# Two transformer blocks in one kernel: unit-matrix products without a use are left out

## The chip, the cores and the metric

One core of a Trainium2 chip. The metric is the device time of one execution in microseconds. Before the change three runs took 3058.13, 3059.27 and 3061.95 us; their median is 3059.27.

## What is computed

Two blocks of two layers each work on one sequence of 512 tokens with 1024 channels, all in float32. The first block's layer is

```
h = rmsnorm(x);  proj = h @ w_in
y_a = gated_delta_branch(...)     # 8 heads, chunks of 64, both directions
y_b = diff_attention_branch(...)  # 8 heads, softmax minus lambda * softmax
x = x + (sigmoid(gate_a) * (y_a @ w_pa) + sigmoid(gate_b) * (y_b @ w_pb)) @ w_out
```

and after its two layers comes a final RMS norm. The second block's layer is

```
z = rms(x) @ w_in
y = concat(windowed attention (8 heads), forgetting attention (4), mLSTM (4))
x = x + y @ w_out
x = x + square(relu(rms(x) @ w_ff1)) @ w_ff2
```

The products that the change leaves out are part of none of this.

## The kernel before

Everything is held transposed: channels on the 128 partitions, tokens along the free dimension. x is eight tiles of 128 x 512. Weights come through `Stream` (line 210): a chunk of 1 MB is loaded, ScalarE rounds it to float32r (the high part), VectorE subtracts to get the low part, and TensorE makes three products of 512 columns per tile: high times high, high times low, low times high (lines 319, 322 and 323, in `Stream.product`).

The program is a sequence of stages, each a Block of its own. At the end of a Block all engines meet, and none goes on before the last has come; this text calls it a border. The order is: start (line 572), then for each layer of the first block delta, merge, attention (`diff_phase`), merge, output; then the final norm; then for each layer of the second block attention (`attention2_phase`) and output with feed-forward (`out_ff_phase`). Some of the next stage's products are pulled ahead of the border, and weights of the next stage are loaded and split before it.

Within a stage TensorE's instructions run in the order in which they are written. Where a long stream of weight products can be cut into pieces, it is a generator, `fill`, and `some(fill, n)` puts n pieces of it between the products of a head, so that TensorE has work while the other engines do theirs. `first_chunk` (line 329) is the start of a stage: its step t takes tile t of the normed h as soon as VectorE has its low part (line 532), two output banks at a time, with a pair of gate products between.

The row sums of the RMS norm are products with a matrix of ones. In the start and in the final norm there are eight of 512 columns (line 431), each behind a square of ScalarE (line 427), with two buffers for the squares. In the output stages GpSimd adds the first squares up (line 465), and TensorE makes two products of 256 columns from the sum (line 470) and two from the last square (line 475); ScalarE then takes logarithm and exponential (lines 483 and 486).

`idle_products` (line 688) makes n products of the unit matrix with itself, 128 columns each, in float32, into a bank that the next real product overwrites or that is free at that point. Nobody reads them. They stand in TensorE's order without any wait of their own, at these places:

- start: 6 behind the row sums (line 605)
- final norm: 8 ahead of the sums and 5 behind them (lines 664 and 667)
- merge: 4 at the end (line 786), four times in the program
- output stage of the first block: 5 at the end (line 946), twice
- feed-forward, first layer of the second block only: 8 ahead of the sums for the next norm and 5 behind them (lines 1044 and 1047)
- delta: 6 (first layer) or 4 (second layer) at the beginning (line 1741), and 5 in the first head, ahead of the wait for the matrix that is to be transposed (line 1646)
- attention of the first block: 4 ahead of the last unit's wait for its weights (line 2273), where a unit is 128 queries of one head
- attention of the second block: 6 at the beginning and 4 at the end (lines 2876 and 2932)

That is 106 products in 21 places.

Of the kernel before, what the change touches and what calls it, by code (L numbers as in the profile page):

```python
# [14 lines left out]
P = 128  # L15
# [556 lines left out]
def start_phase(k, xT_in, positions, cc_in, cx_in, following, pairs, gate_weights):  # L572
# [4 lines left out]
    with ExitStack() as ctx:  # L577
        pos = k.sb(ctx, "pos", [P, SEQ], I32)
        ang = k.sb(ctx, "ang", [P, SEQ], F32)
        tmp = k.sb(ctx, "tmp", [P, 3, SEQ], F32)  # L580
        stats = RowStats(k, k.sb(ctx, "sq", [P, 2, SEQ], F32), 4)
        MAGIC = 1.5 * 2.0 ** 23
        C1 = 6.28125
        C2 = float(np.float32(2 * math.pi - C1))
        C3 = float(2 * math.pi - C1 - float(np.float32(2 * math.pi - C1)))
        with nc.Block() as block:
            @block.sync
            def _(sp):
                sp.dma_start(k.xT[:, :, :], xT_in).then_inc(loaded, 16)
                sp.dma_start(k.cc[:, :], cc_in).then_inc(loaded, 16)  # L590
                sp.dma_start(k.cx, cx_in).then_inc(loaded, 16)
                sp.dma_start(pos[:, :], positions.partition_broadcast(P)).then_inc(loaded, 16)
                gw.load(sp)
                following.prefetch(sp)
                for dst, src in pairs:
                    sp.dma_start(dst, src).then_inc(consts, 16)
                sp.wait_ge(loaded, 64)
                sp.wait_ge(consts, 16 * len(pairs))

            @block.tensor  # L600
            def _(pe):
                pe.wait_ge(loaded, 64)
                for t in range(KT):
                    stats.sum(pe, t)
                idle_products(k, pe, 0, 6)

            @block.vector
            def _(dve):
                chain = Chain(dve, stepd)
                dve.wait_ge(loaded, 64)  # L610
                chain(dve.tensor_copy(tmp[:, 0], pos[:, :]))
                chain(dve.tensor_scalar(ang[:, :], tmp[:, 0], k.cx[:, CX_INVF:CX_INVF + 1], None, ALU.mult))

                for w, shift in enumerate((0.0, math.pi / 2)):
                    chain(dve.tensor_scalar(tmp[:, 0], ang[:, :], 1.0 / (2 * math.pi), shift / (2 * math.pi), ALU.mult, ALU.add))
                    chain(dve.tensor_scalar(tmp[:, 1], tmp[:, 0], MAGIC, None, ALU.add))
                    chain(dve.tensor_scalar(tmp[:, 0], tmp[:, 1], MAGIC, None, ALU.subtract))
                    chain(dve.scalar_tensor_tensor(tmp[:, 1], tmp[:, 0], -C1, ang[:, :], ALU.mult, ALU.add))
                    chain(dve.scalar_tensor_tensor(tmp[:, 1], tmp[:, 0], -C2, tmp[:, 1], ALU.mult, ALU.add))
                    chain(dve.scalar_tensor_tensor(tmp[:, 1], tmp[:, 0], -C3, tmp[:, 1], ALU.mult, ALU.add))  # L620
                    dst = k.sin1 if w == 0 else k.cos1
                    chain(dve.tensor_scalar(tmp[:, 1], tmp[:, 1], shift, math.pi, ALU.add, ALU.min))
                    dve.tensor_scalar(dst[:, :], tmp[:, 1], -math.pi, None, ALU.max).then_inc(posf, 1)
                    dve.wait_ge(posf, w + 1)
                gw.low(dve)
                following.first_low(dve)

            @block.scalar
            def _(act):
                act.preload_act_table_set(LN_EXP)  # L630
                act.wait_ge(loaded, 64)
                for t in range(KT):
                    stats.square(act, t)
                gw.high(act)
                following.first_high(act)
                stats.finish(act)
# [4 lines left out]
def final_norm_phase(k, fn, gain, pairs, gate_weights):  # L641
# [5 lines left out]
    with ExitStack() as ctx:  # L647
        stats = RowStats(k, k.sb(ctx, "sq", [P, 2, SEQ], F32), 4)
        with nc.Block() as block:
# [11 lines left out]

            @block.tensor
            def _(pe):
                idle_products(k, pe, 0, 8)
                for t in range(KT):
                    stats.sum(pe, t)
                idle_products(k, pe, 0, 5)

            @block.scalar
            def _(act):  # L670
# [12 lines left out]
                gw.low(dve)  # L683
                dve.wait_ge(prod, KT)
    k.next_phase()


def idle_products(k, pe, bank, n):

    for _ in range(n):  # L690
        pe.matmul(k.bank[bank][:, 0:P], k.ident, k.ident, start=True, stop=True)


def gate_product(k, pe, w, width, bank, t):
# [48 lines left out]
def merge_phase(k, st, following, yS, macc, mS, begun, pairs=(), angles=()):  # L743
# [5 lines left out]
    with ExitStack() as ctx:  # L749
# [3 lines left out]
        with nc.Block() as block:  # L753
# [12 lines left out]
            @block.tensor  # L766
            def _(pe):
                pe.sem_inc(tile, 1)
                for c in range(2):
                    st.ready(pe, 0, c)  # L770
                    out = k.bank[2 + c if c else begun][:, :]
                    steps = tuple(range(KT)) if c else (KT - 1,)
                    whole(st.product(pe, out, c, 1, yS, frees=c == 1, steps=steps, begin=c == 1)).then_inc(tile, 2 - c)

                with pe.Fori(1, KT // 2) as i:
                    for c in range(2):
                        st.ready(pe, i, c)

                        pe.wait_ge(mul, nth(i, 2, c))
                        whole(st.product(pe, k.bank[c][:, :], c, 0, k.hT)).then_inc(tile, 1)  # L780
                        whole(st.product(pe, k.bank[2 + c][:, :], c, 1, yS)).then_inc(tile, 1)
                if mS is not None:

                    pe.wait_ge(mul, 2 + KT - 1)
                    drain(first_outputs(k, pe, following, OUT_BANKS_MERGE, mS, MERGE_FIRST, lambda t: pe.wait_ge(mul, 3 + t)))
                idle_products(k, pe, 7, 4)

            @block.scalar
            def _(act):
# [139 lines left out]
def out_phase(k, st, following, aS, sq, banks, left, pairs=(), gate_weights=None):  # L929

    out = OutStage(k, st, following, aS, sq, banks + banks, left, pairs, gate_weights)
    with k.nc.Block() as block:
# [9 lines left out]
        @block.tensor  # L942
        def _(pe):
            out.tensor(pe)
            out.sums(pe)
            idle_products(k, pe, 7, 5)

        @block.scalar
        def _(act):
# [20 lines left out]
def out_ff_phase(k, st_out, aS, sq, left, st, following, gain_of, gate_weights=None, pairs=(), result=None):  # L970
# [9 lines left out]
    with ExitStack() as ctx:  # L980
# [5 lines left out]
        with nc.Block() as block:  # L986
# [23 lines left out]
            def _(pe):  # L1010
# [10 lines left out]
                def second(i, c, last_panel):  # L1021
# [16 lines left out]
                    if last_panel and c == 3:  # L1038
# [2 lines left out]
                                step(kk, n)  # L1041
                        if stats:
                            pe.wait_ge(relu, 4 + 4 * NP)
                            idle_products(k, pe, 2, 8)
                            stats.gathered_sum(pe)
                            stats.last_sum(pe)
                            idle_products(k, pe, 2, 5)
                        return
                    for kk in range(4):
                        if c == 2:  # L1050
# [244 lines left out]
def delta_phase(k, st, following, l, pA, cg, tab, lam, yS, wsp, odd, few):  # L1295
# [23 lines left out]
    with ExitStack() as ctx:  # L1319
# [73 lines left out]
        with nc.Block() as block:  # L1393
# [139 lines left out]
            def _(pe):  # L1533
# [108 lines left out]
                def core(i, p, first=False, ahead=2):  # L1642
                    fill = stream(i, ahead)
                    some(fill, 3 if first else 1)
                    if first:
                        idle_products(k, pe, AB + 1, 5)
                    pe.wait_ge(nn_ready, i + 1)
                    for c in range(NS):
                        last = pe.transpose(B[AB][:, c * P:(c + 1) * P], Nn[:, c], k.ident)
# [88 lines left out]
                        turn_out(i, i, "out")  # L1738
                        drain(fill)

                idle_products(k, pe, YB + 1, 4 if l else 6)
                st.ready(pe, 0, 0)
                for last in first_chunk(st, pe, (B[0][:, :], B[1][:, :]), k.hT, norm.ready(pe), gates.product(pe)):
                    last.then_inc(tile, 1)
# [394 lines left out]
def diff_phase(k, st, following, lam, yS, odd):  # L2139
# [22 lines left out]
    with ExitStack() as ctx:  # L2162
# [10 lines left out]
        UNITS1 = HEADS * NTOK  # L2173
# [4 lines left out]
        with nc.Block() as block:  # L2178
# [39 lines left out]
            def _(pe):  # L2218
# [50 lines left out]
                def turn_weights(u):  # L2269
                    if u > 0:  # L2270
                        pe.wait_ge(at_ready, u)
                    if u == UNITS1 - 1:
                        idle_products(k, pe, TB, 4)
                    pe.wait_ge(a_ready, u + 1)
                    for c in range(NTOK):
                        last = pe.transpose(B[TB][:, c * P:(c + 1) * P], A[:, u % 2, c * P:(c + 1) * P], k.ident)
# [403 lines left out]
def attention2_phase(k, st, following, pB, cb, col, yS, wsp, bones, caus, few):  # L2680
# [38 lines left out]
    with ExitStack() as ctx:  # L2719
# [38 lines left out]
        with nc.Block() as block:  # L2758
# [41 lines left out]
            def _(pe):  # L2800
# [72 lines left out]
                                             vtm[:, m % 2, kb, 64 * h:64 * h + 64], start=(y == 0), stop=(y == len(ks) - 1))  # L2873
                    last.then_inc(pv_ready, 1)

                idle_products(k, pe, TB + 1, 6)
                st.ready(pe, 0, 0)
                for last in first_chunk(st, pe, (B[GB], B[GB + 1]), k.hT, norm_in.ready(pe), gates.product(pe)):
                    last.then_inc(g_ready, 1)
# [49 lines left out]
                values(UNITS - 1)  # L2929
                drain(fill)  # L2930
                turn_out(TILES - 1)
                idle_products(k, pe, TB, 4)

            @block.scalar
            def _(act):
# [491 lines left out]
```

## Time and profile before

| what | value |
|---|---|
| median of three runs | 3059.27 us |
| the profiled execution | 3057.0 us |
| its span, first to last instruction | 3055.1 us |
| mean granted clock of TensorE | 0.999 |
| TensorE matmul busy | 2959.6 us, 97% |
| VectorE busy | 1722.9 us, 56% |
| ScalarE busy | 1422.7 us, 47% |
| GpSimd busy | 414.2 us, 14% |
| start stage | 0 to 24.6 us |
| first block, two layers | to 1807 us |
| final norm | to 1819.7 us |
| second block, two layers | to the end |

Busy is the time in which at least one instruction of the engine runs; a matmul's end is modelled, so that a row of eight matmuls in a sequence seems to overlap with the next. The granted clock is that of TensorE's array as a share of 2.4 GHz: 1.00 is 2.4 GHz, 0.50 is 1.2 GHz. All times in the rows are microseconds from the first instruction.

### The profile page before, as it was taken

Reading aid. Unit: us, or ns where it says so; the run is one execution under the profiler, and the core shown is the slowest. Engines: PE = TensorE matmul, PEld = TensorE weight load, DVE = VectorE, ACT = ScalarE, POOL = GpSimd, SP = SyncE. Lnnn points to the kernel's source line nnn. Section 1 sums busy time; section 2 is a strip of 40 time slices with the busy share of each in tenths; the row PEclk is TensorE's granted clock in tenths of the full one; section 3 lists DMA queues with packets and bytes.
Section 4 is the critical chain, followed back from the end, with each engine's and each line's share of the span. In section 5 each row is a group of like instructions: output and inputs, shape, how many; then the busy total and the mean of one; then the engine's idle time right before and its main releaser. Section 6 shows DMA issues by size and latency. Waiting matters only on the chain. (4 is left out here: it accounts for less than half of the span.)

```text
span 3055.1 us, 51528 instructions
## 1 busy us (share of the span) xinstructions
PE 2959.6 (97%) x20560; PEld 2377.1 (78%) x20560; DVE 1722.9 (56%) x2610; ACT 1422.7 (47%) x2790; POOL 414.2 (14%) x276
## 2 busy tenths in 40 slices
PE   7999989999999999899999999999999999999999
PEld 5788768777787887777777777778888877788887
DVE  6767743677437677734776445554444455554444
ACT  4555542665424555533666345653232356633322
POOL 1554510000014445300000010000000100010000
PEclk9999999999999999999999999999999999999999
DMA  4121112221222112122221222213222221122222
GB/s 150 64 75 60 56 63 84 73 74 63 80 87 98 64 64 84 43 70 86 73 73 46 105 86 87 76 37 123 96 96 96 83 87 58 54 97 96 96 96 83
DMA packets 42255, 243.17 MB, mean 80 GB/s; under 512 B 6784, under 2 KB 7744, under 8 KB 16576
## 3 DMA queue, kind: packets, MB, share of 16 engines
q1 hardware_dynamic: 42048, 240.30, 22.2%
q8 instruction: 143, 2.34, 0.3%
q14 instruction: 64, 0.52, 0.1%
HBM read 233.36 MB, written 2.20 MB: 77 GB/s over the span
## 5 line engine op out<-in xcount | busy, mean ns | idle before, releaser
L319 PE MATMUL bank<-hT,ws 128*128 128x512 f32 x2112 | 871.8, 413 | 13.3 <-issue 7.3
L323 PE MATMUL bank<-hT,ws 128*128 128x512 f32 x2112 | 826.3, 391 | 0.0
L322 PE MATMUL bank<-hT,ws 128*128 128x512 f32 x2112 | 824.0, 390 | 0.0
L319 PEld LDWEIGHTS bank<-hT,ws 128*128 128x128 f32 x2112 | 397.3, 188 | 97.7 <-issue 19.3
L270 ACT ACTIVATE ws<-raw 128x2048 fp32r<-128x2048 f32 x172 | 328.9, 1912 | 295.7 <-PE bank L319 178.2
L276 DVE TENSOR_TENSOR ws<-raw,ws 128x2048 fp32r<-128x2048 f32 x160 | 372.8, 2330 | 164.3 <-ACT ws L270 161.3
L323 PEld LDWEIGHTS bank<-hT,ws 128*128 128x128 f32 x2112 | 396.4, 188 | 86.7
L322 PEld LDWEIGHTS bank<-hT,ws 128*128 128x128 f32 x2112 | 398.1, 188 | 68.0 <-issue 1.4
L1031 PE MATMUL bank<-uS,ws 128*128 128x512 f32 x512 | 199.2, 389 | 0.0
L1034 PE MATMUL bank<-uS,ws 128*128 128x512 f32 x512 | 199.2, 389 | 0.0
L1035 PE MATMUL bank<-uS,ws 128*128 128x512 f32 x512 | 199.2, 389 | 0.0
L1950 DVE SCALAR_TENSOR_TENSOR cb<-cb,small 128x512 f32<-128x512 f32 x192 | 181.3, 944 | 4.7
L319 PE MATMUL bank<-yS,ws 128*128 128x512 f32 x384 | 152.4, 397 | 6.2 <-PEq L2758 2.2
L1127 DVE TENSOR_TENSOR xT<-xT,bank 128x512 f32<-128x512 f32 x128 | 87.2, 688 | 113.6 <-PE bank L1035 113.6
L323 PE MATMUL bank<-yS,ws 128*128 128x512 f32 x384 | 149.9, 390 | 0.0
L322 PE MATMUL bank<-yS,ws 128*128 128x512 f32 x384 | 149.8, 390 | 0.0
L465 POOL TENSOR_TENSOR sq<-sq 128x512 f32<-128x512 f32 x18 | 25.4, 1413 | 872.9 <-ACT sq L454 872.9
L1099 ACT ACTIVATE u<-u 128x512 f32<-128x512 f32 x64 | 40.4, 632 | 220.2 <-DVE u L1120 220.2
L2350 ACT ACTIVATE pr<-bank,odd 128x512 f32<-128x512 f32 x128 | 86.7, 682 | 112.0 <-DVE odd L2424 112.0
L2424 DVE TENSOR_REDUCE odd<-bank 128x1 f32<-128x512 f32 x128 | 82.3, 685 | 83.2 <-PE bank L2264 83.1
L465 POOL TENSOR_TENSOR macc<-macc 128x512 f32<-128x512 f32 x12 | 25.3, 2109 | 762.3 <-ACT macc L454 762.3
L1120 DVE SCALAR_TENSOR_TENSOR u<-bank,row_scale 128x512 f32<-128x512 f32 x64 | 44.0, 690 | 148.8 <-PE bank L323 148.8
(368 smaller groups left out, 4854.1 us busy)
## 6 DMA issues: line engine op xcount, KB each, us to landing
raw<-in_w_ff SPq DMA_DIRECT2D x64, 1024.0 KB, 4.7
raw<-in_w_delta SPq DMA_DIRECT2D x32, 1024.0 KB, 4.8
raw<-in_w_diff SPq DMA_DIRECT2D x32, 1024.0 KB, 4.7
raw<-in_w_att SPq DMA_DIRECT2D x20, 1024.0 KB, 4.8
raw<-in_w_merge_a SPq DMA_DIRECT2D x16, 1024.0 KB, 4.7
raw<-in_w_merge_b SPq DMA_DIRECT2D x16, 1024.0 KB, 4.7
raw<-in_w_out SPq DMA_DIRECT2D x16, 1024.0 KB, 4.9
rows<-sum_rows SPq DMA_DIRECT2D x16, 512.0 KB, 5.6
```

Of the source, the lines that this page charges most:

```text
L270: act.activation(self.k.ws[:, c % 2, 0], self.k.raw[:, c % 2], ACT.Copy).then_inc(self.high_done, 1)
L276: dve.tensor_tensor(self.k.ws[:, c % 2, 1], self.k.raw[:, c % 2], self.k.ws[:, c % 2, 0].bitcast(F32), ALU.subtract).then_inc(self.low_don ...
L319: first = pe.matmul(out, hi, x[:, 0, k], start=(begin and k == steps[0]), stop=False)
L322: pe.matmul(out, hi, x[:, 1, k], start=False, stop=False)
L323: last = pe.matmul(out, lo, x[:, 0, k], start=False, stop=(end and k == steps[-1]))
L1031: first = pe.matmul(o, hi, uS[:, 0, kk], start=(kk == 0), stop=False)
L1034: pe.matmul(o, hi, uS[:, 1, kk], start=False, stop=False)
L1035: last = pe.matmul(o, lo, uS[:, 0, kk], start=False, stop=(kk == 3))
L1127: dve.tensor_tensor(k.xT[:, n], k.xT[:, n], k.bank[4 + n % 4][:, :], ALU.add).then_inc(added, 1)
L1950: ins = dve.scalar_tensor_tensor(cv[:, j], pad[:, j, w:w + SEQ], cw[:, j, w:w + 1], cv[:, j], ALU.mult, ALU.add)
L2350: act.activation(pr[:, u % 2, m], B[SB + m][:, :], ACT.Exp, bias=sc[:, u % 2, m:m + 1], accum_out=sc[:, u % 2, 2 + m:3 + m]).then_inc(p_re ...
L2424: dve.tensor_reduce(sc[:, u % 2, m:m + 1], B[SB + m][:, :], AX_X, ALU.max, negate=True).then_inc(max_ready, 1)
```

## The change

All calls of `idle_products` are taken out, and the helper with them. Nothing else differs: no wait, no transfer, no order of other instructions.

```diff
@@ start_phase, tensor
                 for t in range(KT):
                     stats.sum(pe, t)
-                idle_products(k, pe, 0, 6)
@@ final_norm_phase, tensor
-                idle_products(k, pe, 0, 8)
                 for t in range(KT):
                     stats.sum(pe, t)
-                idle_products(k, pe, 0, 5)
@@
-def idle_products(k, pe, bank, n):
-
-    for _ in range(n):
-        pe.matmul(k.bank[bank][:, 0:P], k.ident, k.ident, start=True, stop=True)
@@ merge_phase, tensor
                     drain(first_outputs(k, pe, following, OUT_BANKS_MERGE, mS, MERGE_FIRST, lambda t: pe.wait_ge(mul, 3 + t)))
-                idle_products(k, pe, 7, 4)
@@ out_phase, tensor
             out.tensor(pe)
             out.sums(pe)
-            idle_products(k, pe, 7, 5)
@@ out_ff_phase, tensor, second
                         if stats:
                             pe.wait_ge(relu, 4 + 4 * NP)
-                            idle_products(k, pe, 2, 8)
                             stats.gathered_sum(pe)
                             stats.last_sum(pe)
-                            idle_products(k, pe, 2, 5)
@@ delta_phase, tensor, core
                     some(fill, 3 if first else 1)
-                    if first:
-                        idle_products(k, pe, AB + 1, 5)
                     pe.wait_ge(nn_ready, i + 1)
@@ delta_phase, tensor
-                idle_products(k, pe, YB + 1, 4 if l else 6)
                 st.ready(pe, 0, 0)
@@ diff_phase, tensor, turn_weights
                         pe.wait_ge(at_ready, u)
-                    if u == UNITS1 - 1:
-                        idle_products(k, pe, TB, 4)
                     pe.wait_ge(a_ready, u + 1)
@@ attention2_phase, tensor
-                idle_products(k, pe, TB + 1, 6)
                 st.ready(pe, 0, 0)
@@ attention2_phase, tensor, end
                 turn_out(TILES - 1)
-                idle_products(k, pe, TB, 4)
```

## Rows read from the trace of the kernel before

**Rows 1.** The page: busy us (share of the span) x instructions, TensorE.

```profile
PE 2959.6 (97%) x20560; PEld 2377.1 (78%) x20560; DVE 1722.9 (56%) x2610; ACT 1422.7 (47%) x2790; POOL 414.2 (14%) x276
```

**Rows 2.** Instructions of line 691: count, min/median/max ns, first and last start, form.

```profile
L691 PE MATMUL bank<-cc x212: 270/275/348, 20.8 to 2664.1; 128*128 128x128 f32 x106
```

**Rows 3.** Windows: from:to, length, busy (instructions) of PE PEld DVE ACT POOL, clock, DMA.

```profile
1972.02:1975.41 3.39, 3.39 (x18) 3.37 (x16) 3.16 (x8) 1.44 (x5) 0.00 (x0) 0.50 0.03 5
2634.20:2637.60 3.40, 2.84 (x11) 2.36 (x10) 3.29 (x5) 0.65 (x3) 0.00 (x0) 0.50 0.01 2
3050.00:3054.00 4.00, 0.00 (x0) 0.00 (x0) 0.49 (x1) 0.00 (x0) 0.00 (x0) 1.00 0.17 66
3054.05:3055.00 0.95, 0.00 (x0) 0.00 (x0) 0.00 (x0) 0.00 (x0) 0.00 (x0) 0.50 0.00 0
```

**Rows 4.** TensorE in order: start, length, engine line op [idle before, releaser], around the falls.

```profile
1970.38 0.49 PE L2858 MATMUL bank<-qk 64*128 64x128 f32 x4 [1.48 <-DVEq L3194]
...
1972.04 1.91 PE L2920 MATMUL bank<-cc,Sm 128*128 128x128 f32 x8
...
1975.81 0.48 PE L319 MATMUL bank<-hT,ws 128*128 128x512 f32 x1
...
2632.61 0.87 PE L2920 MATMUL bank<-cc,Sm 128*128 128x128 f32 x6 [1.66 <-ACT Sm L2983]
...
2639.51 1.10 PE L2920 MATMUL bank<-cc,Sm 128*128 128x128 f32 x8 [0.28 <-ACT Sm L2983]
...
2641.73 0.61 PE L2836 MATMUL bank<-cc,rq 128*128 128x128 f32 x4
```

**Rows 5.** Instructions in order at the last unit of attention and a merge's border.

```profile
782.65 0.75 DVE L2432 SCALAR_TENSOR_TENSOR pr<-pr,odd 128x512 f32<-128x512 f32 x1
...
784.26 1.05 PE L691 MATMUL bank<-cc 128*128 128x128 f32 x8
...
785.15 0.60 PE L2276 MATMUL bank<-cc,pr 128*128 128x128 f32 x4
...
879.16 0.47 PE L319 MATMUL bank<-mS,ws 128*128 128x512 f32 x1 [0.30 <-PEq L753]
```

**Rows 6.** Instructions in order at the other places, by time.

```profile
20.78 1.50 PE L691 MATMUL bank<-cc 128*128 128x128 f32 x12
...
24.76 1.58 PE L691 MATMUL bank<-cc 128*128 128x128 f32 x12 [2.48 <-PEq L586]
...
26.55 0.47 PE L319 MATMUL bank<-hT,ws 128*128 128x512 f32 x1 [0.21 <-DVE hT L532]
...
76.69 0.66 PE L1649 MATMUL bank<-cc,Nn 128*128 128x128 f32 x4 [1.04 <-DVE Nn L2014]
...
515.45 0.47 PE L319 MATMUL bank<-hT,ws 128*128 128x512 f32 x1 [1.13 <-PEq L753]
...
914.66 1.13 PE L475 MATMUL bank<-macc,cc 128*128 128x256 f32 x4 [0.36 <-ACT macc L454]
...
916.20 0.68 ACT L486 ACTIVATE bank<-macc 128x256 f32<-128x256 f32 x2
...
919.13 0.47 PE L319 MATMUL bank<-hT,ws 128*128 128x512 f32 x1 [0.65 <-DVE hT L532]
...
1804.67 1.13 PE L475 MATMUL bank<-macc,cc 128*128 128x256 f32 x4 [0.37 <-ACT macc L454]
...
1810.33 7.70 PE L431 MATMUL bank<-sq,cc 128*128 128x512 f32 x16 [1.10 <-ACT sq L427]
...
1821.88 0.47 PE L319 MATMUL bank<-hT,ws 128*128 128x512 f32 x1 [0.46 <-DVE hT L532]
...
2048.04 0.47 PE L319 MATMUL bank<-yS,ws 128*128 128x512 f32 x1 [1.11 <-PEq L2758]
...
2435.23 1.13 PE L470 MATMUL bank<-sq,cc 128*128 128x256 f32 x4 [1.12 <-POOL sq L465]
```

**Rows 7.** Window of line 431 alone at the start: PE and PEld busy (instructions), clock.

```profile
11.90:16.20 4.30, 4.30 (x6) 1.58 (x5) 1.00 1.01 419
```

## The prediction

> **What bounds the kernel now.** I read five views in this order. The page first: TensorE's matmul row is busy for 97% of the span [rows 1]. The kernel is one queue of products, and every microsecond in which that queue stands or runs at half clock is a microsecond of the span, unless something else would have ended the stretch anyway. Then the instructions of the helper's line: 106 idle products are 212 matmul rows [rows 2], because each float32 product of 128 columns is two passes. Eight rows in a row take 1.05 us with the tail of the last one, and the next matmul starts 0.89 us after the first of them [rows 5], so a row costs 0.11 us and a product 0.22 us. All 106 are 24 us of TensorE, under 1% of the span. Third, the granted clock by windows: in the whole program it falls twice, at 1972.0 and at 2634.2, each time for 3.4 us, and once more after the last product [rows 3]. Fourth, TensorE's own order of time around those falls [rows 4]. Fifth, the order of time around each of the 21 places (calls times layers) where idle products stand, for one question: what released the instruction behind them [rows 5, 6].
>
> **What is taken out, and what it gives back.** Nothing is added or moved; no wait, transfer or buffer changes. An idle product gives time back only where TensorE is the last to be ready. The rows sort the places into two kinds.
>
> Four places are on the path. In the last unit of the attention of the first block (784.3, and the same at 1674.3) the products stand between the stream and the transposes of the weights. VectorE's last instruction on those weights ends at 783.40, before the first idle product starts at 784.26, and the transposes go at 785.15 with no gap [rows 5]. Without the products they go at 784.26 or so: 0.89 us each. At the end of the two merges that hand over to the output stage (877.8, and the same at 1767.8) TensorE is the last to reach the border: the next stage's first product comes only 0.30 us after its last idle row [rows 5], where other borders take 0.5 to 1.1 us [rows 6]. Without them the border opens 8 x 0.11 = 0.89 us earlier. Sum of the four: 3.6 us. Its lower end is 0, if another engine's arrival at the border or the copy behind the transposes is late instead; the rows show neither, so I take the full 3.6.
>
> All the other places give nothing. At the end of the output stages ScalarE's last exponentials end at 916.88, as late as the idle products, and open the border; behind the border the first product waits for hT, which is ready later than the idle products are done [rows 6]. At the two merges before the attention (515.45), and behind the second block's attention (2048.04), the border opens 1.1 us after the last idle row, so another engine is last; in the first head of the delta stage the transposes still wait 1.04 us for VectorE, until 76.69; in the feed-forward the sum waits for GpSimd until 2435.23 [rows 6]. Were one of these covers a little shorter than it looks, the gain would be tenths of a microsecond.
>
> **What the products keep away: empty TensorE.** With them gone, these stops appear, from the end of the last real matmul to the start of the next [rows 6]: 5.6 us at the first border (20.9, where the first idle products start, to 26.55), 3.3 us at the next layer's border (915.79 to 919.13), 4.5 us ahead of the final norm (1805.80 to 1810.33), 3.9 us behind it (1818.03 to 1821.88), and 3.6 us at the second layer of the second block, which repeats the pattern of the one at 915.79. That is five long ones. For the others the stop is the idle products' own 0.11 us a row and the wait behind them. A middle kind: 2.9 us ahead of the sums of the feed-forward (16 rows and 1.12 us, until 2435.23), and twice 2.0 us behind the thin end of the second block's attention (8 rows and 1.11 us, until 2048.04, and the same at 2665.5). Short ones: 2.1 us at the first head of each delta stage (10 rows and 1.04 us, until 76.69; the same at 969.3) and 2.0 us at the first merge (until 515.45).
>
> Which of them make the clock fall? The rows give three falls to measure by. After the last product of the program the clock stays at 2.4 GHz for 4 us of nothing, until 3054.0 [rows 3]. Before the fall at 1972.0 TensorE stood for 1.48 us and then had only a few narrow products and one sum; before the one at 2634.2 it had stood for 1.66 us [rows 4]. So thin stretches suffice. On the other side the stop of 2.48 us at the first border, with 1.3 us of idle products either side, was followed by no fall [rows 6]. I count the five long stops as certain (5.0), the three middle ones at 0.75 each (2.25) and the three short ones at 0.35 each (1.05): 8.3 new falls. The bounds are 2 (only the stops longer than 4 us) and 11 (all of them).
>
> The Trainium skill, page "TensorE: Matmul & The Clock Gate", section "What's actually happening", says that the clock goes to half after a stretch in which TensorE is idle throughout, which speaks against most of this count. The trace disagrees: two falls came after stretches with matmuls in them [rows 4]. [...] The same page, in the part on the PE-mode transpose, says that transposes don't count as activity in the way that matmuls do; by that the two stops behind the attention, which follow transposes, would be certain, 0.5 fall or 0.8 us more.
>
> **What one fall costs.** The first one can be priced by equal work. Eight transposes and twelve value products take 3.77 us from 1972.04 to 1975.81, most of it at 1.2 GHz, and 2.22 us from 2639.51 to 2641.73 at 2.4 GHz [rows 4]: 1.55 us lost. The other way to it: the stretch of 3.4 us at half clock [rows 3] holds 1.7 us less work if TensorE is the bound throughout. What follows each of the new stops is dense: the first chunk of a stage (each step of eight products is fed by VectorE faster than it is eaten) or, in the final norm, sums of two passes that TensorE paces. I take 1.6. From below: 0.8, if half of the slow stretch lies in waits. From above: 2.6, half of the 5.2 us from the first sum at 11.0 to 16.2 at the start, in which five weight loads of the sums take 4.3 us, 0.86 us a pass, against 0.48 in the final norm, waits included (the clock column reads 1.00 there, the spacing says 1.2 GHz) [rows 6, 7]. A stop also slows the waits' chains a little; I put no number on that.
>
> **The sum.** The profiled execution took 3057.0 us (span 3055.1, and 1.9 around it), with two falls that stay in place. 3057.0 - 3.6 + 8.3 x 1.6 (13.3) = 3066.7; I say 3066, since two falls close together can merge. The median of the runs shown is 3059.27, so the change comes to 6.7 us or 0.22% slower. That median lies 2.3 us above the profiled execution, which reads as one or two falls more in thin places. I don't add it to the forecast, as some of those places are among the eleven; I do add it to the rivals that leave them alone.
>
> **Rivals.**
> 1. *Long stops alone.* The clock falls at the five long stops and at none of the others. For it: the 2.48 us stop in the rows brought no fall. Against it: the falls after 1.5 and 1.7 us of standing. 3057.0 + 2.3 - 3.6 + 5 x 1.6 = 3063.7.
> 2. *Only wholly empty stretches.* Two falls (the stops of 5.6 and 4.5 us, both longer than the 4 us behind the last product). 3057.0 + 2.3 - 3.6 + 2 x 1.6 = 3058.9. Against it: the same two falls of rows 4.
> 3. *Faster: the path is all there is.* The idle products never held the clock; the four places give their 3.6 us and nothing is given back: 3057.0 + 2.3 - 3.6 = 3055.7, 0.12% under the median. It decides as soon as fewer than 3.6 / 1.6 = 2.2 new falls come. For it: 106 products are under 1% of the work. Against it: the fall at 3054.0 after 4 us of nothing, and a stop of 5.6 us that the change opens.
> 4. *Slow recovery.* After a long stop the clock needs as long as at the start of the program: 8.3 x 2.6 = 21.6, so 3057.0 - 3.6 + 21.6 = 3075. For it: the first sums [rows 7]. Against it: both falls inside the program lasted 3.4 us.
>
> **How the numbers follow.** Forecast 0.53, long stops alone 0.20, only empty stretches 0.12, faster path 0.07, slow recovery 0.08. A measurement of this kernel tells about 0.2% (6 us) from no change, that is 3053.2 to 3065.4 count as the same. The forecast's own range is 3062 to 3070; six sevenths of it I count as slower (0.45), with the slow recovery (0.08) and the upper edge of rival 1 (0.03): 0.56. Faster by over 0.2% is only the far end of rival 3 and of the executions' spread: 0.04. The same: 0.40. The range for 8 in 10 goes from 3058 (rival 2 and the forecast's low end) to 3073.
>
> **What would show it.** In the changed kernel's profile the mean clock falls and half-clock stretches of 3.4 us or more appear right behind the stops at 26, 919, 1810, 1822 and 2440, and in about half of the other six; each step of a first chunk behind them has its products at about twice the usual distance. The transposes at 784 and 1674 start 0.9 us sooner after the stream's last product, and the two merge borders shorten by 0.9 us. Other borders keep their length to 0.1 us. I am wrong if the clock column stays full behind the stops of 3 to 4 us (rival 2), if it falls but the stage's end doesn't move (the slow stretch lay in waits), or if the slow stretches last 5 us (rival 4).

## The result, and the profile after

The changed kernel is slower. Its median is 3073.72 us (3070.37 to 3076.48) against 3059.68 us for the kernel before beside it: a ratio of 1.0044, 95% interval 1.0032 to 1.0056. The forecast was 3066, its range ended at 3073.

The profiled execution took 3070.45 us (span 3068.6 us), so 13.5 us more than the profiled one of before. TensorE's busy time fell by 10 us where the idle products alone had held some 24 [rows 1, 2]: the work that is left takes 14 us more. The page, part 1 and the costliest group of part 5:

```profile
PE 2949.4 (96%) x20348; PEld 2360.6 (77%) x20348; DVE 1723.2 (56%) x2610; ACT 1422.0 (46%) x2790; POOL 412.6 (13%) x276
...
L319 PE MATMUL bank<-hT,ws 128*128 128x512 f32 x2112 | 876.1, 415 | 29.7 <-DVE hT L532 16.4
```

In the whole program the granted clock now falls 11 times, and two of the falls last two times 3.4 us: at 25.5, 80.1, 452.1, 923.2, 974.4, 1291.8, 1814.0, 1831.1, 1851.6, 2445.5 and 2452.3. Before it fell at 1972.0 and 2634.2 [rows 3]. In units of 3.4 us that is 13 against 2. Five of the windows, in the columns of [rows 3]:

```profile
25.40:32.20 6.80, 5.77 (x14) 4.35 (x15) 6.70 (x12) 3.58 (x7) 2.04 (x2) 0.50 0.47 154
80.10:83.40 3.30, 3.30 (x15) 2.16 (x16) 1.67 (x3) 0.00 (x0) 2.34 (x3) 0.50 0.00 0
452.20:455.50 3.30, 3.30 (x9) 2.55 (x8) 1.25 (x2) 1.91 (x1) 0.00 (x0) 0.50 0.77 243
...
1814.10:1820.80 6.70, 4.26 (x5) 1.80 (x6) 5.36 (x8) 2.97 (x5) 0.00 (x0) 0.50 0.60 190
...
2445.60:2448.90 3.30, 2.90 (x7) 1.74 (x6) 0.00 (x0) 1.02 (x3) 0.00 (x0) 0.50 0.00 0
```

TensorE in order behind the first border, the first head of the delta stage, a place that never had idle products, and the final norm (start, length, line, idle before and releaser):

```profile
26.43 0.77 PE L319 MATMUL bank<-hT,ws 128*128 128x512 f32 x1 [5.61 <-DVE hT L532]
26.99 0.63 PE L322 MATMUL bank<-hT,ws 128*128 128x512 f32 x1
27.42 0.63 PE L323 MATMUL bank<-hT,ws 128*128 128x512 f32 x1
...
32.11 0.47 PE L323 MATMUL bank<-hT,ws 128*128 128x512 f32 x1
32.42 0.39 PE L689 MATMUL bank<-hT,yS 128*64 128x512 f32 x1
32.65 0.40 PE L690 MATMUL bank<-hT,yS 128*64 128x512 f32 x1
...
79.14 0.66 PE L1634 MATMUL bank<-cc,Nn 128*128 128x128 f32 x4 [2.12 <-DVE Nn L1998]
...
80.11 0.63 PE L323 MATMUL bank<-hT,ws 128*128 128x512 f32 x1
80.53 0.63 PE L319 MATMUL bank<-hT,ws 128*128 128x512 f32 x1
...
449.48 0.39 PE L323 MATMUL bank<-yS,ws 128*128 128x512 f32 x1
451.82 0.50 PE L319 MATMUL bank<-hT,ws 128*128 128x512 f32 x1 [1.95 <-issue]
452.13 0.62 PE L322 MATMUL bank<-hT,ws 128*128 128x512 f32 x1
452.55 0.63 PE L323 MATMUL bank<-hT,ws 128*128 128x512 f32 x1
...
1816.54 9.64 PE L431 MATMUL bank<-sq,cc 128*128 128x512 f32 x16 [4.39 <-ACT sq L427]
...
1830.03 0.47 PE L319 MATMUL bank<-hT,ws 128*128 128x512 f32 x1 [3.84 <-DVE hT L532]
```

The first product behind the first border starts at 26.43, as early as before (26.55) [rows 6]: the stop of 5.6 us itself costs nothing. But the products then come 0.43 us apart until 32.1, and 0.23 apart after it. The sums of the final norm take 9.64 us instead of 7.70 [rows 6].

Two of the four places on the path (the other two repeat them): VectorE's last work on the weights and the transposes behind it, then the merge's border:

```profile
788.07 0.75 DVE L2414 SCALAR_TENSOR_TENSOR pr<-pr,odd 128x512 f32<-128x512 f32 x1
```

```profile
789.68 0.49 PE L2258 MATMUL bank<-cc,pr 128*128 128x128 f32 x3
...
882.12 0.39 PE L323 MATMUL bank<-mS,ws 128*128 128x512 f32 x1
882.82 0.47 PE L319 MATMUL bank<-mS,ws 128*128 128x512 f32 x1 [0.30 <-PEq L744]
```

The transposes start 0.86 us after VectorE's end at 788.82; before it was 1.75 [rows 5]. The border comes 0.70 us after the start of the merge's last product; with the idle row it was 1.58.

**Where the time went.** Each VectorE instruction of after was set beside the same one of before, and the steps in the difference of their starts were added up. Gains: 0.89 at 784, 0.90 at 878, 0.89 at 1674, 0.87 at 1768, together 3.6 us. Losses at the 11 falls: 2.6 at 25, 1.5 at 80, 1.6 at 452, 1.4 at 923, 1.6 at 974, 1.5 at 1292, 1.8 at 1814, 1.4 at 1831, 1.6 at 1852, 1.7 and 1.4 at 2445 and 2452: 18.1 us. The fall at 1972, gone, gives back 1.6, the one at 2634 gives back nothing that can be seen, 0.7 is lost in small steps behind 2475 (the largest is 0.9 lost at 2504, where the clock is full in both), and two steps of 0.1 are gained elsewhere. That makes 18.1 - 1.6 + 0.7 - 0.2 - 3.6 = 13.4 us, the difference of the two executions.

### The profile page after: what moved, and what is told of

Its sections match the earlier page's. It is cut to its first block and busy times, and to the rows that moved or that the text cites. A ratio compares the mean times of both kernels' runs of the same rounds, so it can differ in the third digit from the quotient of the medians.

```text
span 3068.6 us, 51107 instructions
## 1 busy us (share of the span) xinstructions
PE 2949.4 (96%) x20348; PEld 2360.6 (77%) x20348; DVE 1723.2 (56%) x2610; ACT 1422.0 (46%) x2790; POOL 412.6 (13%) x276
```

## Experiments

Theory: the idle products hold the clock through covered waits, and the time lost follows the time at half clock. Rivals: the loss comes from the stops themselves, or from the path places; only long stops count; only real matmuls hold the clock, or only wholly empty stretches lower it.

"Half clock" below is the mean over a kernel's executions of (1 - mean clock) x 2 x span, the tail behind the last product (0.3 to 3 us in the traces) included. The clock is recorded to 0.001, so that one execution's value is known to 3 us only and the means are what counts. For the kernel before it is 14.8 us over the 90 executions made beside the experiments, with a mean time of 3059.7 us: its typical execution has about two falls more than the profiled one (7.9 us). For the changed kernel it is 54.1 us over 5 executions, with a mean of 3073.2.

Ratios are to the runs of before made beside each kernel, and so are the differences of means in the text. These runs differ a little among themselves: beside e1 to e4 the kernel before has a mean of 3060.3 us and 15.5 us of half clock (24 executions), beside e5 to e8 3059.2 and 12.0 (33), beside e9 to e12 3059.8 and 17.1 (33).

| kernel | idle products | median us | mean us | ratio (95%) | half clock us |
|---|---|---|---|---|---|
| before | 106 | 3059.6 | 3059.7 | 1 | 14.8 |
| after | 0 | 3073.7 | 3073.2 | 1.0044 (1.0032, 1.0056) | 54.1 |
| e1_path_out | 90 | 3060.3 | 3060.8 | 1.0002 (0.9993, 1.0011) | 21.1 |
| e8_path_out_again | 90 | 3059.3 | 3060.0 | 1.0003 (0.9994, 1.0012) | 17.8 |
| e11_attention_path_out | 98 | 3060.4 | 3060.2 | 1.0002 (0.9993, 1.0011) | 13.9 |
| e12_merge_path_out | 98 | 3060.8 | 3060.6 | 1.0006 (0.9997, 1.0015) | 18.9 |
| e2_covered_out | 16 | 3075.6 | 3075.7 | 1.0051 (1.0038, 1.0065) | 52.9 |
| e3_long_out | 50 | 3068.4 | 3068.3 | 1.0027 (1.0016, 1.0037) | 39.1 |
| e4_short_out | 72 | 3067.2 | 3067.6 | 1.0027 (1.0018, 1.0036) | 29.5 |
| e7_half | 50 (half each) | 3065.8 | 3065.8 | 1.0020 (1.0011, 1.0029) | 33.4 |
| e6_transposes | 106 as 212 transposes | 3057.0 | 3057.3 | 0.9995 (0.9986, 1.0004) | 8.3 |
| e5_more_cover | 188 | 3057.9 | 3057.7 | 0.9995 (0.9986, 1.0004) | 8.9 |
| e9_cover_fixed | 197 | 3053.6 | 3054.3 | 0.9983 (0.9974, 0.9992) | 7.2 |
| e10_cover_transposes | 197 as 394 transposes | 3054.2 | 3055.1 | 0.9986 (0.9977, 0.9996) | 7.8 |

**e1_path_out, and the same kernel again as e8_path_out_again.** Only the 16 products of the four path places go.

```diff
-                idle_products(k, pe, 7, 4)
+                if mS is None:
+                    idle_products(k, pe, 7, 4)
...
-                    if u == UNITS1 - 1:
-                        idle_products(k, pe, TB, 4)
```

> Only the 16 products at the four places where TensorE is the last to be ready are left out (the last unit of the first block's attention, the end of the two merges ahead of the output stage); the other 90 stay. Theory A (the idle products hold the clock, and each lost fall has its price): no new fall, since the stops that open are 0.3 us long; 4 x 0.89 = 3.6 us faster than before, ratio 0.9988. Rival B (the whole 13.5 us of the change come from these places too, for example from a border that is then opened by a slower engine): not faster. Either theory: half-clock time as in the kernel before.

> The kernel without the 16 products on the path once more, beside the others of this call. The first time its trace had all four gains of 0.9 us, but its median was that of the kernel before, with 21 us of half clock on average against 15.6. Theory A (the excess of half-clock time was chance): now 2 to 3.6 us faster. Rival D (the products on the path hold the clock too, so that leaving them out gives back in falls what it gains): again the same, with more half-clock time than before.

Neither is faster: 1.0002 and 1.0003. Set beside the kernel before, the traces show each local gain (0.88, 0.89, 0.90 and 0.87 us in e1; 0.88, 0.89, 0.88 and 0.85 in e8). Their executions spread more widely, with a standard deviation of 3.9 and 3.0 us against 2.1, and have 5.6 and 5.8 us more at half clock than the runs beside them. That is what rival D of the second expectation foresaw, at least in part: at 0.24 to 0.44 us per us of half clock (both prices stand further down) it takes back 1.4 to 2.5 of the 3.6 us. The trace of e1 has falls at 25.8, 2012.4, 2585.8 and 2630.2, none beside the four places; the one of e8 has one at 1969.3, close to the one of before. A fall in a thin stretch of e1, TensorE in order:

```profile
2010.92 0.87 PE L2919 MATMUL bank<-cc,Sm 128*128 128x128 f32 x6 [1.66 <-ACT Sm L2982]
...
2013.20 1.09 PE L2845 MATMUL bank<-cc,cb 128*128 128x128 f32 x4 [0.46 <-DVE cb L3206]
...
2014.51 0.63 PE L322 MATMUL bank<-yS,ws 128*128 128x512 f32 x1
2014.94 0.63 PE L323 MATMUL bank<-yS,ws 128*128 128x512 f32 x1
```

It is the pattern of [rows 4]: a wait of 1.66 us among small products, then 0.43 us a product. Nothing of the change is near it, and it costs little: what stands behind it comes 0.1 us later. So the local gain is real, and the step from it to the time of the kernel failed.

**e2_covered_out.** The opposite: the 90 covered products go, the 16 on the path stay.

```diff
-                idle_products(k, pe, 7, 4)
+                if mS is not None:
+                    idle_products(k, pe, 7, 4)
```

and each other call but the one in `turn_weights` is taken out.

> The complement: the 90 products at the 17 covered places are left out, the 16 on the path stay. Theory A: the whole loss of the change without its gain, 13.5 + 3.6 = 17.1 us slower than before, ratio 1.0056, mean granted clock 0.990 to 0.992. Rival B (the clock has no part): 0 us, since nothing on the path changes. If it is about 12 us only, the falls in thin places that the change doesn't touch (near 450, 1290, 1850, 2452 in the changed kernel's trace) were chance.

3075.6 us: the whole loss, and 2 us more than the full change. The path places have no part in the loss. Price: (3075.7 - 3060.3) / (52.9 - 15.5) = 0.41 us per us of half clock. Against the changed kernel the path's gain does show: 2.5 us between the means, with a standard error of 1.2.

**e3_long_out.** Out: the 56 products around the five long stops (the calls of the start, the final norm, the output stages, the end of the feed-forward, and the two ahead of the first chunks).

```diff
-                idle_products(k, pe, 0, 6)
...
-                idle_products(k, pe, 0, 8)
...
-                idle_products(k, pe, 0, 5)
...
-            idle_products(k, pe, 7, 5)
...
-                            idle_products(k, pe, 2, 5)
...
-                idle_products(k, pe, YB + 1, 4 if l else 6)
...
-                idle_products(k, pe, TB + 1, 6)
```

> Only the 56 products around the five long stops (3.3 to 5.6 us) are left out. Theory A: the shifts read in the changed kernel's trace at these five, 2.6 + 1.4 + 1.8 + 1.4 + 1.7 = 8.9 us slower, ratio 1.0029, five falls at the same places. Rival C (only wholly empty stretches longer than 4 us count): two falls, 3.2 us, ratio 1.0010. Rival B: 0.

Mean +8.0 us, with 23.6 us more at half clock. The trace has a fall at each of the five (26.8, 921.1, 1815.4, 1829.0, 2446.8) and four in thin places (450.0, 2023.6, 2481.0, 2644.8).

**e4_short_out.** Out: the 34 others that are covered.

```diff
-                idle_products(k, pe, 7, 4)
+                if mS is not None:
+                    idle_products(k, pe, 7, 4)
...
-                            idle_products(k, pe, 2, 8)
...
-                    if first:
-                        idle_products(k, pe, AB + 1, 5)
...
-                idle_products(k, pe, TB, 4)
```

> Only the 34 products at the short and middle stops (2.0 to 2.9 us: the first head of delta, the sums of the feed-forward, the two merges ahead of attention, the end of the second block's attention) are left out. Theory A, as the forecast counted them: 3 x 0.75 + 3 x 0.35 = 3.3 falls, 5 us; as the changed kernel's trace shows them: two falls, 1.5 + 1.6 = 3.1 us, ratio 1.0010. Rival C: 0, no stop here is longer than 3 us. Together with the run without the long stops' products it should give the run without all covered ones; what is missing in the sum is what the parts do to each other.

Mean +7.3 us, with 14.0 us more at half clock, so more than the forecast's count gives. Of the seven stops that open here (1.6 to 3.0 us), three are followed by a fall in the trace. TensorE around the first head, the end of the second block's attention and the sums of the feed-forward, and the windows behind:

```profile
78.12 0.66 PE L1647 MATMUL bank<-cc,Nn 128*128 128x128 f32 x4 [2.13 <-DVE Nn L2012]
...
79.36 0.63 PE L319 MATMUL bank<-hT,ws 128*128 128x512 f32 x1
...
2050.00 0.63 PE L2844 MATMUL bank<-cc,cb 128*128 128x128 f32 x4 [0.70 <-ACT cb L3003]
2052.63 0.77 PE L319 MATMUL bank<-yS,ws 128*128 128x512 f32 x1 [2.00 <-PEq L2756]
...
2441.24 1.19 PE L470 MATMUL bank<-sq,cc 128*128 128x256 f32 x2 [3.00 <-POOL sq L465]
```

```profile
79.30:82.50 3.20, 3.20 (x23) 2.09 (x25) 1.44 (x3) 0.00 (x0) 2.24 (x3) 0.50 0.00 0
2052.20:2055.40 3.20, 2.77 (x7) 2.23 (x8) 0.69 (x1) 1.67 (x2) 0.00 (x0) 0.50 0.54 133
2441.40:2444.60 3.20, 3.20 (x8) 2.57 (x9) 0.00 (x0) 0.94 (x3) 0.00 (x0) 0.50 0.00 0
```

Stops of 2.0 to 3.0 us are enough, so "long stops alone" and "only wholly empty stretches" both fall. The other falls in this trace (451.3, 1857.6, 2021.4, 2598.3) lie where the kernel before has no idle products either. The two halves add up: 8.0 + 7.3 = 15.3 us, against 15.4 in e2.

**e7_half.** Every call issues half its products: `range(n // 2)`.

> Half of the products at every place (rounded down, 52 of 106 products stay). Path gain 1.8 us. If the loss goes with the emptied time: half of 17.1, so 17.1 / 2 - 1.8 = 7 us slower. If half of them is enough to hold the clock at most places: about -1.8 us. Theory A expects something between, since stops of 5.6 and 4.5 us stay half empty while those of 2 us are then 1 us long: 3 to 5 us slower, 2 to 4 falls more than before.

Mean +6.6 us. (Rounded down place by place, 50 products stay, not the 52 of the expectation.) With the path's half, 1.8 us, added back, 8.4 us of loss over 21.4 us more half clock is 0.39. In its trace the clock falls for two units of 3.4 us at 24.6, 1813.2 and 2052.2, for one at 922.4 and 2448.1 and at two thin places (451.3, 2021.4), and not behind the first head at 80. Half the cover protects the short stops in part and the long ones hardly.

**e6_transposes.** Each idle product (two passes of float32) becomes two transposes of the same unit matrix.

```diff
-    for _ in range(n):
-        pe.matmul(k.bank[bank][:, 0:P], k.ident, k.ident, start=True, stop=True)
+    for _ in range(2 * n):
+        pe.transpose(k.bank[bank][:, 0:P], k.ident, k.ident)
```

> Each idle product is replaced by two transposes of the unit matrix (128 columns, one pass each), so that the same number of rows of about 0.11 us stands at the same places; nothing else differs. If transposes hold the clock as products do: 0 us, half-clock time as before (about 15 us). If they don't count, as a page of the Trainium skill has it: the 3.6 us of the path stay and the covered places fall as if they were empty, 15 to 17 us slower, clock 0.991.

They hold the clock as well: half clock 8.3 us against 12.0, 3057.0 us against 3058.89 beside it, a difference within what can be told apart. The helper's line before, as weight loads, and then with transposes, as weight loads and matmuls (count, min/median/max ns):

```profile
L691 PEld LDWEIGHTS bank<-cc x212: 186/192/192, 20.4 to 2664.0; 128*128 128x128 f32 x106
...
L691 PEld LDWEIGHTS bank<-cc x212: 138/140/230, 20.0 to 2662.7; 128*128 128x128 f32 x106
L691 PE MATMUL bank<-cc x212: 270/272/421, 20.5 to 2662.8; 128*128 128x128 f32 x106
```

As many passes, as long as before (270/275) [rows 2], only the weight loads are shorter. Of the two kinds of product tried, either holds the clock.

**e5_more_cover.** If falls in thin places are most of what is left, covering them must pay. To e1 are added idle products at each merge, in the last head's step of the delta stage, and in two thin units of the second block's attention:

```diff
+                idle_products(k, pe, 7, 8 if mS is None else 6)
...
+                        if i == HEADS - 1 and a > 0:
+                            idle_products(k, pe, AB + 1, 3)
...
+                    if u in (19, 26):
+                        pe.wait_ge(at_ready, u)
+                        idle_products(k, pe, TB, 6 if u == 19 else 5)
...
+                    if u in (26, 27):
+                        pe.wait_ge(at_ready, u)
+                        idle_products(k, pe, TB, 6)
```

> The 16 products on the path are out, the 90 covered ones stay, and more are added where the traces show TensorE waiting in thin places: 8 or 6 in each merge between its first two and its next products (waits of 1.97 and 1.63 us), 3 ahead of each level but the first in the delta stage's last head (waits of 0.7 us), 5 or 6 at four waits of the second block's attention (waits of 1.2 to 1.7 us, units 19, 26, 27). Theory A: the executions of the kernel before hold 15.6 us of half clock on average and each microsecond costs 0.45 us; with most of the falls gone 4 to 5 us come back beside the 3.6 of the path: about 3052 us, ratio 0.9973, clock 0.998 to 0.999. Rival B (these waits are shorter than the products in them, so that they land on the path): same as before, or slower, at a higher clock.

Half clock down by 3.2 us to 8.9, mean down 1.5 us, ratio 0.9995: not separate from no change. The trace shows one of the new covers on the path, the one at the second layer's first merge:

```profile
1342.27 1.95 PE L691 MATMUL bank<-cc 128*128 128x128 f32 x16
1343.97 0.48 PE L319 MATMUL bank<-hT,ws 128*128 128x512 f32 x1
```

Sixteen rows, and the next product follows without a gap; set beside the kernel before, the following instructions come 1.8 us later. Before, TensorE has no wait there at all.

**e9_cover_fixed.** e5 without that cover, and with longer ones in the waits that have room.

```diff
-                idle_products(k, pe, 0, 6)
+                idle_products(k, pe, 0, 14)
...
-                idle_products(k, pe, 0, 8)
+                idle_products(k, pe, 0, 12)
...
+                if angles or mS is not None:
+                    idle_products(k, pe, 7, 8 if mS is None else 6)
...
-                            idle_products(k, pe, 2, 8)
+                            idle_products(k, pe, 2, 13)
...
-                        idle_products(k, pe, AB + 1, 5)
+                        idle_products(k, pe, AB + 1, 9)
...
+                            idle_products(k, pe, AB + 1, 2)
```

> The kernel with more cover once more, with its fault mended: the 8 products in the second layer's first merge, where its trace showed no wait and 2.0 us on the path, are out, and the delta stage's fills are 2 products long in place of 3. Four covers are made longer, up to what their waits hold: start 14, ahead of the final norm's sums 12, first head 9, feed-forward 13. Theory A: the mended kernel had 3057.7 us on average (half clock 8.9 us); 2 us less on the path and one fall less: 3055 us, ratio 0.9985, clock 0.999 or more. Rival B (the longer covers land on the path now): again 3058.

3053.64 us (3053.39 to 3057.93), 0.9983 with an interval below 1: with nearly twice the idle products it beats both kernels, as only its twin e10 below does too. Mean half clock 7.2 us, 9.8 less than beside it. The place where e1 fell at 2013 is now, TensorE in order:

```profile
2010.92 1.60 PE L691 MATMUL bank<-cc 128*128 128x128 f32 x12
2012.36 0.82 PE L2929 MATMUL bank<-cc,Sm 128*128 128x128 f32 x6
```

Here the path's gain shows in the time. At the same recorded clock, 0.999, nine executions of e9 average 3053.7 us and the five of before beside them 3056.9: 3.2 of the 3.6 us. The fastest executions lie 2.4 us apart (3053.4 and 3055.8).

**e10_cover_transposes.** e9 with the edit of e6.

> The same kernel with every idle product as two transposes. The transposes had 3057.3 us and 8.3 us of half clock on average at the first kernel's places, against 59.7 and 13.7 for products. If transposes hold the clock at least as well: the same as the run beside it or up to 1 us less, about 3054.5. If that difference was chance: equal.

3054.19 us, half clock 7.8 against 7.2 us: the same as e9. With transposes or matmuls, the cover works alike.

**e11_attention_path_out and e12_merge_path_out.** The two halves of e1: in e11 only the call in `turn_weights` goes, in e12 only the one of the merges with `mS`.

> Of the 16 products on the path only the 8 in the first block's attention are left out, all others stay. Theory A: 1.8 us faster than before, 3057.9 against an average of 3059.7. Rival D (products on the path hold the clock too): 0, or slower, with half-clock time above the 13.7 us of before.

> Of the 16 products on the path only the 8 at the ends of the two merges are left out. Theory A: 1.8 us faster than before, 3057.9. Rival D: 0, or slower, with more half-clock time than before. Whichever of this and the run beside it is not faster is where the gain of the path goes.

Both missed: 1.0002 and 1.0006 where each should have gained 1.8 us. Their traces show the local gains again (0.89 and 0.89 in e11; 0.89 and 0.87 in e12), and neither median moves. The means are 0.5 and 0.9 us over that of before, with a standard error of 1.0 and 0.9. e11 has 3.1 us less at half clock than the runs beside it, so that rival D doesn't hold for it, and with the 1.8 us of the path it should take 3059.8 - 1.8 - 3.1 x 0.24 = 3057.3 us, or less by the higher price. It takes 3060.2, three standard errors more.

The traces show one thing that takes gain back and is no fall. Behind each of the two borders after the second block's attention ScalarE waits for the next weights. In order: the border (ScalarE's table load) and the rounding of the weights before, in e8 with TensorE's wait behind it, and in e9:

```profile
2048.00 1.28 ACT L887 ACT_TABLE_LOAD   x1 [1.33 <-PEq L2758]
...
2053.51 1.92 ACT L270 ACTIVATE ws<-raw 128x2048 fp32r<-128x2048 f32 x1 [2.53 <-DMA raw<-in_w_out]
```

```profile
2045.28 1.28 ACT L888 ACT_TABLE_LOAD   x1 [1.33 <-PEq L2757]
...
2051.56 1.92 ACT L270 ACTIVATE ws<-raw 128x2048 fp32r<-128x2048 f32 x1 [3.29 <-DMA raw<-in_w_out]
...
2058.32 0.47 PE L319 MATMUL bank<-yS,ws 128*128 128x512 f32 x1 [0.50 <-DVE ws L276]
```

```profile
2044.91 1.28 ACT L890 ACT_TABLE_LOAD   x1 [1.33 <-PEq L2761]
...
2049.76 1.92 ACT L270 ACTIVATE ws<-raw 128x2048 fp32r<-128x2048 f32 x1 [1.88 <-DMA raw<-in_w_out]
```

From the one to the other it takes 5.5 us before, 6.3 in e8 and 4.9 in e9. At the two borders of e1, e8, e11 and e12 it is 5.7 and 6.2, 6.3 and 6.5, 6.1 and 6.2, 5.3 and 6.5; in the nine other changed kernels it is 4.8 to 5.0 at 16 of the 18 borders and 5.7 and 5.8 at the other two. Wherever it is over 6 us, TensorE stands 0.4 to 0.7 us for VectorE's part of these weights, and what follows comes 0.6 to 1.0 us later. Added up over both borders, that is 0.7 us in e1, 1.7 in e8, 1.3 in e11 and 0.9 in e12 of the 3.5 or 1.8 gained. Why the transfer lands later in just these four kernels, and whether it does in all their executions, is not shown: each has one trace. With it the trace of e8 closes: 3.5 us gained on the path, 0.7 lost at the start, ahead of any edit, and 1.7 here make 1.1 of the 1.2 us that it is faster than the traced execution of before. For the means of the four kernels the rest stays open.

## Why the prediction was wrong

The direction, the mechanism and two of the three sizes held. The step that failed is the count: "8.3 new falls" of one stretch of 3.4 us each, on top of "two falls that stay in place", was taken for the whole change in slow time. The runs show 11 stretches net in its place. Beside it failed the choice "I don't add it to the forecast", which left out the 2.3 us between the profiled execution and the median.

- **Path gain, 3.6 us.** In the trace it was 3.6, each of the four 0.87 to 0.90. Between the changed kernel and e2 2.5 us of it show in the time. Taken alone it doesn't show in four kernels, which the lower end of 0 allowed for, though by another reason than the ones named.
- **The other 17 places give nothing.** No border among them opens earlier in the trace of after, and e2 without the covered products gains nowhere.
- **Where the clock falls.** Eight of the eleven stops had a fall, so for these places 8.3 was right: all five long ones (25, 923, 1814, 1831, 2452), one of the middle ones (2445) and both first heads (80, 974). At two of them (25 and 1814) the clock stayed down for 6.8 us, in part what the rival *slow recovery* foresaw; so the eight are ten units of 3.4 us. A twelfth stop, the second merge ahead of attention (1.6 us, until 1413.6), was missing from the list and had none.
- **What was not counted.** Three more falls (452, 1292, 1852) lie outside the list, at places where the kernel before has no idle products, against two before (1972 and 2634), which were to stay and are both gone. Net: 10 + 3 - 2 = 11 units, not 8.3. That they come with either kernel is seen in e12, which has all the covered products and falls at 451.4 and 1287.7.
- **The price, 1.6 us a fall.** The size was right: 18.1 us over 11 falls is 1.65, over 13 units 1.4. From the means of all executions the price is (3073.2 + 3.6 - 3059.7) / (54.1 - 14.8) = 0.44 us per us of half clock, 1.5 us for 3.4. It is the price of a fall in dense work. Among the 90 executions of the kernel before the time rises by only 0.24 us per us of half clock (24 with a recorded clock of 0.999 average 3057.3 us, 21 with 0.996 average 3061.7), 0.8 us for 3.4: its falls lie in thin stretches for a part, and of the two in its trace one is worth 1.6 us and the other nothing.
- **From the profiled execution to the median.** The profiled 3057.0 us lie 2.7 us under the median of before. That execution had two falls where the typical one has four (14.8 us of half clock, less the tail), and the executions with its recorded clock, 0.999, average 3057.3 us. The changed kernel's profiled execution, too, lies 3.3 us under its median, and its half clock 8 us under the mean of its five. So the 2.3 us seen belonged in the forecast.

The two together: the losses of the accounting are 18.1 - 1.6 + 0.7 - 0.2 = 17.0 us, and 3057.0 - 3.6 + 17.0 = 3070.4 is the profiled execution; 3.3 us more is the median. Of the 7.0 us between 3066.7 and 3073.7 the count has 17.0 - 13.3 = 3.7, and the choice of the start 3.3.

The number that came closest, 3075 of *slow recovery*, was near by luck: it takes 2.6 us for each of 8.3 falls. That cost was measured at one fall only (25); the other ten cost 1.4 to 1.8.

Of the rivals, *long stops alone* and *only wholly empty stretches* fell by e4, *faster* by e2. The Trainium skill, page "TensorE: Matmul & The Clock Gate", section "What's actually happening", says the clock drops behind a stretch idle throughout; here stops of 2.0 to 3.0 us with real matmuls either side were enough (e4). Its part on the PE-mode transpose says that a transpose doesn't count as busy in the same way; e6 and e10 show transposes holding the clock, with 8.3 and 7.8 us of half clock against 12.0 and 7.2 with matmuls.

## What to carry to other kernels

Count filler products by what they hold, not by what they occupy: behind a wait they cost nothing and keep TensorE at full clock, on the path they cost their own length. Find the places by the granted clock over windows, of more than one execution, since a stretch with a stop of 1.5 us or more falls in one and not in the next; a microsecond at half clock cost 0.4 us here where dense work followed the stop, and 0.24 us among the executions of the kernel before. And look whether the profiled execution is a typical one before a sum starts from it.

## What was not expected of the hardware

- Where a fall lands differs between executions of nearly the same kernel. The stop of 2.5 us at the first border has a fall in e1, e5, e6 and e12 (at 24.7 to 26.3 us), and none in before, e4, e8 or e11; all have the same instructions there, but for e6 with its transposes.
- Behind a long stop the clock can stay down for 6.8 us, even where products follow each other densely from the first us on, as at 26.43 above; in e3, whose start is the same as the changed kernel's, it stays down for 3.4 us only.
- The kernel before was not free of this: 107 more idle products in waits, with the 16 on the path left out (e9), take the kernel from 17.1 to 7.2 us of half clock and its mean down by 5.5 us, of which some 3 are the path's, by the comparison at equal clock above.
- The weights behind the second block's attention reach ScalarE 4.8 to 6.5 us behind the border in different traces, though no edit touches that transfer (under e12). At six borders it was over 6 us, and each of them cost 0.6 to 1.0 us.
